# A hybrid encoder block on one core: the last output projection in one row of matmuls, both tiles' transposes and expert choices behind it

## The reference

```python
x = x + merged @ w_out[l]
x = x + moe_ffn(rms_norm(x, norm_ffn[l]), w_router[l], b_router[l], w_gate[l], b_gate[l], w_up[l], b_up[l], w_down[l], b_down[l])
...
logits = (xt @ w_router + b_router).astype(jnp.float32)
top_val, top_idx = lax.top_k(logits, TOP_K)
wts = jax.nn.softmax(top_val, axis=-1)
...
g = xblk @ w_gate[e] + b_gate[e]
u = xblk @ w_up[e] + b_up[e]
...
return act @ w_down[e] + b_down[e]
```

## Time and profile before

| | before |
|---|---|
| median of 3 runs | 1459.51 us (1458.72 to 1461.27) |
| the profiled execution: its own time | 1459.15 us |
| its span, first to last instruction | 1457.0 us |
| TensorE busy | 1426.1 us (98%) |
| VectorE busy | 592.2 us (41%) |
| ScalarE busy | 405.9 us (28%) |
| GpSimd busy | 63.5 us (4%) |
| granted TensorE clock, mean | 1.000 |
| data moved | 491.27 MB, mean 337 GB/s |

### The profile page before, as it was taken

The page is one execution under the profiler, slowest core; times in us unless marked ns, Lnnn a source line. Parts: engine busy times, 40 slices in busy tenths (PEclk is TensorE's granted clock), DMA queues, the critical chain, the costliest instruction groups (busy, mean ns, idle before and its releaser), DMA issues.

```text
span 1457.0 us, 18622 instructions
## 1 busy us (share of the span) xinstructions
PE 1426.1 (98%) x7575; PEld 820.1 (56%) x7575; DVE 592.2 (41%) x1149; ACT 405.9 (28%) x601; POOL 63.5 (4%) x50
## 2 busy tenths in 40 slices
PE   6999999999999999999999999999999999999998
PEld 6898888777778873444444444444444444433443
DVE  6779788787778552112121121211112111111111
ACT  5766666556535441010110110001011010101110
POOL 5110000111100000000000000000000000000000
PEclk9999999999999999999999999999999999999999
DMA  7455444654563969999999999999999999999996
GB/s 248 153 186 177 155 138 161 196 160 160 173 244 131 379 261 423 428 428 427 429 428 430 428 429 428 429 429 428 429 428 429 428 429 428 429 428 429 428 427 287
DMA packets 74001, 491.27 MB, mean 337 GB/s; under 512 B 5265, under 2 KB 8977, under 8 KB 49377
## 3 DMA queue, kind: packets, MB, share of 16 engines
q1 hardware_dynamic: 71280, 487.57, 82.8%
q10 hardware_dynamic: 2160, 2.62, 0.6%
q0 software_dynamic: 512, 0.43, 0.2%
HBM read 488.93 MB, written 1.07 MB: 336 GB/s over the span
## 4 chain that ended last, share of the span: by engine, by line
PE 80%; DMA 10%; DVE 6%; ACT 2%; issue 2%; DVEq 0%; ACTq 0%; SPq 0%
PE ps L1929 26%; PE ps L1967 13%; PE ps L1590 7%; PE ps L1857 7%; PE ps L1592 7%; PE ps L1591 7%; DMA regions<-in_w_up 6%; PE ps L1577 4%; PE ps L1909 4%; DMA regions<-in_w_gate 3%; DVE regions L1165 2%; DVE splits L1019 2%; PE ps L1804 1%; ACT splits L706 1%; PE ps L1937 1%
## 5 line engine op out<-in xcount | busy, mean ns | idle before, releaser
L1929 PE MATMUL ps<-regions,sig 128*64 128x512 f32 x2048 | 463.4, 594 | 4.5 <-DMA regions<-in_w_gate 4.2
L1929 PEld LDWEIGHTS ps<-regions,sig 128*64 128x64 f32 x2048 | 141.9, 137 | 277.1 <-issue 259.5
L1967 PE MATMUL ps<-regions,tmp 128*64 128x512 f32 x1024 | 225.1, 592 | 0.0
L1590 PE MATMUL ps<-splits,regions_r 128*128 128x512 f32 x512 | 205.8, 402 | 1.9 <-DVE regions_r L1012 1.7
L1592 PE MATMUL ps<-splits,regions_r 128*128 128x512 f32 x512 | 200.1, 391 | 0.0
L1591 PE MATMUL ps<-splits,regions_r 128*128 128x512 f32 x512 | 199.8, 390 | 0.0
L706 ACT ACTIVATE splits<-halves 128x1024 fp32r<-128x1024 f32 x152 | 159.1, 1056 | 100.2 <-PE ps L1592 83.4
L1019 DVE TENSOR_TENSOR splits<-halves,splits 128x1024 fp32r<-128x1024 f32 x132 | 166.0, 1262 | 46.5 <-ACT splits L706 45.1
L892 ACT ACTIVATE work<-work 128x512 f32<-128x512 f32 x32 | 20.1, 629 | 475.4 <-DVE work L1517 475.4
L1967 PEld LDWEIGHTS ps<-regions,tmp 128*64 128x64 f32 x1024 | 71.8, 137 | 131.9 <-issue 129.5
L1857 PEld LDWEIGHTS ps<-craw,regions 128*128 128x128 f32 x1024 | 119.2, 192 | 25.6 <-issue 25.2
(11 more groups left out here) (299 smaller groups left out, 1186.3 us busy)
## 6 DMA issues: line engine op xcount, KB each, us to landing
regions<-in_w_gate SPq DMA_DIRECT2D x64, 2048.0 KB, 29.7
regions<-in_w_up SPq DMA_DIRECT2D x64, 2048.0 KB, 28.0
regions<-in_w_down SPq DMA_DIRECT2D x64, 2048.0 KB, 30.9
halves<-in_w_in SPq DMA_DIRECT2D x48, 1024.0 KB, 5.2
halves<-in_w_br_b SPq DMA_DIRECT2D x8, 1024.0 KB, 5.1
halves<-in_w_mem_kv SPq DMA_DIRECT2D x8, 1024.0 KB, 5.0
halves<-in_w_br_a SPq DMA_DIRECT2D x4, 1024.0 KB, 7.5
halves<-in_w_br_c SPq DMA_DIRECT2D x4, 1024.0 KB, 7.5
```

The lines of the kernel that those rows point to most:

```text
L1590: pe.matmul(out, lhs[0], rhs[0], start=start, stop=False, skip_group_check=True)
L1929: last = pe.matmul(ps[64 * h:64 * h + 64, bank, :], xgT[:, 4 * k + c], eslots[slot][:, c, h * NB:(h + 1) * NB], start=(k == 0 and c == 0), ...
L1967: last = pe.matmul(ps[64 * h:64 * h + 64, D_BANK, :], actT[:, c, 64 * k:64 * k + 64], eslots[slot][:, c, h * NB:(h + 1) * NB], start=False ...
```

## The change

The four quarters of the second tile are now steps of the list: `second(0)` and `second(1)` behind unit first("wo", 1) + 1, `second(2)` and `second(3)` behind the last unit. So PE's projection is one row of 48 matmuls: the first tile's quarters 0 and 1, the second tile's 0 and 1, then the same of quarters 2 and 3. `outT` and `logits` come behind it, `outT` with both `turn_out` groups in it. On DVE the step `outT` begins with `add_out(0)`, `norm_begin(0)`, `norm_end(0)` (the root's inversion, split from `choose`) and `add_out(1)`; then come all copies, `norm_begin(1)`, `norm_end(1)`, `choose(0)`, `find_first(0)`, `choose(1)`. PE waits for `logits_taken` of tile 0 before `last_logits(1)`. The router's weights are scaled (`router_scale`) behind unit first("bc", 0) + 1 in place of with ("wo", 0). No instruction of a tile is added or left out, and the streams of ACT and SP are the same. The diff, cut (the functions `add_out`, `take_xT`, `norm_begin`, `second_tile` and `turn_out` only move up in the file, unchanged):

```diff
     at(first("wo", 1), "picks")
-    at(first("wo", 1) + 2, "outT")
-    at(first("wo", 1) + 3, "logits")
+    for q in range(2):
+        at(first("wo", 1) + 1, "second", q)
+        at(first("wo", 1) + 3, "second", q + 2)
+    at(UNITS, "outT")
+    at(UNITS, "logits")
+    at(first("bc", 0) + 1, "router_scale")
...
+            def norm_end(t):
+
+                inverse_root(rs_2[:, t:t + 1]).then_inc(sem("second_norm"), 1)
+                dve.wait_ge(sem("second_norm"), t + 1)
...
+                elif kind == "router_scale":
+
                     dve.wait_ge(gain2_landed, 32)
...
                 elif kind == "outT":
+                    add_out(0)
+                    norm_begin(0)
+                    norm_end(0)
+                    add_out(1)
                     for c2 in range(2):
...
             def choose(t):
 
-                inverse_root(rs_2[:, t:t + 1]).then_inc(sem("second_norm"), 1)
-                dve.wait_ge(sem("second_norm"), t + 1)
                 dve.wait_ge(sem("logits_ready"), t + 1)
...
-            add_out(0)
             take_xT(0)
-            norm_begin(0)
-            choose(0)
-            add_out(1)
             take_xT(1)
             norm_begin(1)
+            norm_end(1)
+            choose(0)
             find_first(0)
             choose(1)
...
+                elif kind == "second":
+                    second_tile(step[1])
...
                     for c2 in range(2):
                         by_columns(lambda t: x_sb[:, t], c2)
+                    turn_out(0)
+                    turn_out(1)
...
-            second_tile(0)
-            turn_out(0)
-            second_tile(1)
             last_logits(0)
-            second_tile(2)
-            second_tile(3)
-            pe.wait_ge(gemm_taken, GEMM_AT[("wo", 1, 0)] + 1)
+            pe.wait_ge(gemm_taken, GEMM_END)
             open_sum(0, 0)
-            turn_out(1)
+            pe.wait_ge(sem("logits_taken"), 1)
+            last_logits(1)
 
             b = group()
             pe.wait_ge(sem("chosen_ready"), 1)
             pe.matmul(ps[:, b, 0:EXPERTS], upto_r[:], chosen_r[:, 0], start=True, stop=True).then_inc(misc_ready, 1)
-            pe.wait_ge(gemm_taken, GEMM_END)
             open_sum(1, 0)
-            last_logits(1)
```

More of the change, by code:

```diff
@@ L967, in rstd_here, with add_out, take_xT, norm_begin @@
                 return last
+            across = [P, TOP_K, EXPERTS]
+            def add_out(t):
+                n = GEMM_AT[("wo", 1, t)]
+                if t == 0:
+                    dve.wait_ge(sem("wo_first_tile"), 1)
+                else:
+                    dve.wait_ge(unit_used, UNITS)
+                dve.tensor_tensor(x_sb[:, t, NB:2 * NB], x_sb[:, t, NB:2 * NB], ps[:, GEMM_BANKS[n % 4], :], ALU.add)\
+                    .then_inc(gemm_taken, 1)
+            def take_xT(t):
+                b = group()
+                dve.tensor_copy(xT[:, 4:8, t * P:(t + 1) * P], ps[:, b, :].rearrange("p (c t) -> p c t", c=4))\
+                    .then_inc(misc_taken, 1)
+            def norm_begin(t):
+                dve.wait_ge(sem("out_squares"), TT + t + 1)
+                link(dve.tensor_tensor(ss_2[:, t:t + 1], ss_part[:, t:t + 1], ss_part[:, TT + t:TT + t + 1], ALU.add))
+                variance(rs_2[:, t:t + 1], ss_2[:, t:t + 1], D)
+            def norm_end(t):
+                inverse_root(rs_2[:, t:t + 1]).then_inc(sem("second_norm"), 1)
+                dve.wait_ge(sem("second_norm"), t + 1)
             dve.wait_ge(sem("masks"), 3)
@@ L1599, in router, with second_tile, turn_out @@
                 return last
+            def second_tile(q):
+                w = first("wo", 1) + q
+                hi, lo = quarter(w)[1:]
+                b = GEMM_BANKS[GEMM_AT[("wo", 1, 1)] % 4]
+                for c in range(2):
+                    k = 2 * q + c
+                    last = three_passes(ps[:, b, :], (mergedT[0][:, k, P:T], mergedT[1][:, k, P:T]),
+                                        (hi[:, c], lo[:, c]), k == 0, k == KC - 1)
+                last.then_inc(unit_used, 1)
+            def turn_out(t):
+                b = group()
+                pe.wait_ge(gemm_taken, GEMM_AT[("wo", 1, t)] + 1)
+                for c in range(4):
+                    last = turn(ps[:, b, c * P:(c + 1) * P], x_sb[:, t, (4 + c) * P:(5 + c) * P])
+                last.then_inc(misc_ready, 1)
             pe.wait_ge(sem("masks"), 3)
@@ L1826, in _ @@
                         by_columns(lambda t: merged[:, t], c2)
-            def second_tile(q):
-                w = first("wo", 1) + q
-                hi, lo = quarter(w)[1:]
-                b = GEMM_BANKS[GEMM_AT[("wo", 1, 1)] % 4]
-                for c in range(2):
-                    k = 2 * q + c
-                    last = three_passes(ps[:, b, :], (mergedT[0][:, k, P:T], mergedT[1][:, k, P:T]),
-                                        (hi[:, c], lo[:, c]), k == 0, k == KC - 1)
-                last.then_inc(unit_used, 1)
-            def turn_out(t):
-                b = group()
-                pe.wait_ge(gemm_taken, GEMM_AT[("wo", 1, t)] + 1)
-                for c in range(4):
-                    last = turn(ps[:, b, c * P:(c + 1) * P], x_sb[:, t, (4 + c) * P:(5 + c) * P])
-                last.then_inc(misc_ready, 1)
             def last_logits(t):
```

17 lines of the change are left out of this document (removed).

## The result

| | before | after |
|---|---|---|
| median of the runs shown with the result | 1459.35 us (20 runs, 1458.36 to 1461.27) | 1466.07 us (20 runs, 1459.58 to 1472.85) |
| ratio, 95% interval | | 1.0039 [1.0028, 1.0051] |
| profiled execution | 1459.15 us, mean clock 1.000 | 1471.44 us, mean clock 0.991 |

What follows compares the result with a forecast made beforehand. It took a full-rate stream of expert loads, paced from the expert loop's start, as the bound. 1459.15 + 1.5 for new waits, other terms at 0, gave 1460.65, or 1461.0 against the median; range 1458.9 to 1463.6.

Steps and rivals of the forecast that it cites:

- The clock: In the rearranged stretch behind the projection the granted clock was to stay full at 2.4 GHz, with no loss taken.
- Rival D: The clock falls to 1.2 GHz behind the new wait, costing 6 to 12 us, 1467 to 1473 us; chance 0.02.
- Size of a fall: Some 12.5 us of PE work between 529.2 and 543.4 at 1.2 GHz would cost 6 to 12 us.
- load (2, 2): Ninth load of the expert stream, held until PE frees its slot; taken as the later limit by about 0.3 us.
- The new wait: Before turn_out(1), PE idles 1.2 us because add_out(1) and the copies stand behind tile 0's root on DVE.
- The root of tile 0: On ACT behind the projection, the root follows its table load at once at 529.2, freeing DVE about 530.4.
- rival A: Tile 0's root comes later still, delaying the add, copies, router and loop: up to 1463.3 us; chance 0.13.
- At full clock: Waits between projection and gathers make take_gathered, the expert loop and the end 1.5 us later.
- The early load (1, 0): On SP's queue this load goes 5.5 us earlier but gains nothing, hidden behind the slot of load (2, 2).
- One to one: At the expert loop, any later start moves the kernel's end by the same amount, here 1.5 us.
- the stream's start: Rival limit on the expert loads: earlier loads would carry the end up to 3.9 us earlier, 1455.6; chance 0.04.

Runs made afterwards that it cites:

- F4: The kernel before with two more TensorE waits, for tile 1's squares before the first open_sum and tile 1's norm before open_sum(1, 0): 1469.45 us, ratio 1.0062.
- F1: The changed kernel with twelve extra transposes (result unused) in TensorE's wait before turn_out(1): 1466.85 us, ratio 1.0039.
- E1: The changed kernel with two extra 512-column matmuls (four passes, result unused) between turn_out(0) and turn_out(1): 1459.96 us, ratio 1.0010.
- F3: The kernel before with 28 extra transposes in a row behind the projection's last matmul: 1461.02 us, ratio 1.0012.
- G2: The kernel before with 16 extra router products (32 passes of 32 columns) behind the projection's last matmul: 1461.37 us, ratio 1.0015.
- K1: G1 with open_sum(0, 0) moved into the wait before turn_out(1) and open_sum(0, 1) between the router's products: 1463.53 us, ratio 1.0025.
- G1: The changed kernel with its four open_sum placed singly between the router's products and the ranks, no work added: 1461.18 us, ratio 1.0017.
- J1: E1 with load (1, 0) released together with load (1, 1), 5.5 us later: 1460.36 us, ratio 1.0003.
- E5: The kernel before with one more TensorE wait, for tile 1's squares before its first open_sum: 1460.86 us, ratio 1.0013.
- J2: The kernel before with load (1, 0) released together with load (1, 1), some 3.6 us later: 1461.50 us, ratio 1.0013.
- A2: The changed kernel again, with no edit, on another chip: 1467.71 us, ratio 1.0044.
- E2: The changed kernel with DVE's add_out(1) and the two outT copies moved ahead of norm_end(0): 1467.79 us, ratio 1.0062.
- E3: The changed kernel with outT's eight transposes back between the projection's units and the router's first eight products ahead of turn_out: 1467.45 us, ratio 1.0054.
- G3: As E3, with the router's first eight products inside the projection too: 1465.76 us, ratio 1.0035.
- H4: The changed kernel with E1's two extra matmuls right behind the projection, ahead of all transposes: 1461.84 us, ratio 1.0026.
- F2: The changed kernel with open_sum(0, 0) and open_sum(0, 1) moved into the wait before turn_out(1): 1466.89 us, ratio 1.0043.

## Why the prediction was wrong

**The clock: the step that failed.** The prediction took no loss there, with the reasons that the granted clock "remains so where transposes, router and short waits alternate, in the very stretch that is rearranged", and that eight transposes in a row had shown no fall. Both sentences are true of before and neither says how near that stretch stood to a fall. F4 shows it: two waits more, in the unchanged order, and five of six runs fall. Rival D had the mechanism with its size, 1467 to 1473 us "behind the new wait"; the falling runs measured 1466.04 to 1472.85. It got a chance of 0.02, and 11 of 20 runs were of that kind: the term that the sum put at nothing measured 5.7 to 12.5 us in each of them (above the median of the full-clock runs), with the clock at 0.50 from 536.4 to about 556.9 in the one that was profiled. The range to 1463.6 left it out.

What the row of eight transposes could not show is the sum of the parts. The old order lays the light work between matmuls of the projection and puts an `open_sum` between any two of the router's and the transposes' groups. The new order puts the projection ahead, and behind it come 16 transposes, 24 router passes (12 products), and only then the first 512-column passes, with 1.31 us of idleness in the midst. The Trainium skill ("TensorE: Matmul & The Clock Gate", "Part 4: PE-mode transpose") says that transposes don't count for the clock as matmuls do. By that rule the prediction should have given rival D far more. F1, with twelve more transposes in the wait and 8 falls in 12, agrees with it against E1; F3 and G2, with 3 us of nothing but thin work and no fall, show that it decides nothing by itself.

**Size of a fall.** The prediction had "half of it again and more, 6 to 12 us". The fall of the profiled execution lasts from 536.4 to about 556.9. I had let it end at 543.4, the forecast start of the loop; it takes in both gathers and the first products of expert 0 as well. At +5.7 to +12.5 against the full-clock median 1460.39 the runs cover the whole of that. F1's profiled execution against E1's gives 8.3 us at load (2, 2) and 9.7 in the whole time for such a fall of 20 us. K1's fall of 10 us began later and cost less; of G1's falls no trace was taken.

**The new wait: right.** Predicted: 1.2 us of idleness before `turn_out(1)`, released by DVE's first copy, behind an `add_out(1)` that starts 1.2 us after the projection's end. Measured: 1.31, released by L1407, with the add at 531.68 and the projection's end at 530.24, 1.4 ahead of it. That end was forecast at 529.2; in this execution the short fall at 434 us moved all that follows, so the differences are to be compared, not the times.

**The root of tile 0: right, and rival A falls.** The root starts at 530.47, right behind its table load (529.18 + 1.28), so nothing is hidden in the 1.84 us of the earlier trace rows. The Trainium skill ("ScalarE: Activation LUTs", "What ACT_TABLE_LOAD costs") puts a drain of 1.38 us behind such a load; this row shows none, as the earlier trace rows at 540.49 had not.

**At full clock: near, with one term missing.** +1.5 us was forecast. The nine full-clock runs gave 1460.39, +1.04 against the median before, and E1, at the same point of the order, +1.14. The early load (1, 0) is worth nothing (J1), as said. The forecast put load (2, 2) near 570.2, and E1 has it at 570.29. What came out smaller is the step from there to the end.

**One to one: wrong by about a microsecond of slack.** I had written that the end hangs on the loop's start "microsecond for microsecond", since the slot of load (2, 2) was the later of two limits "by a little". In the profiled executions with full clock from 530 us on, the time stands behind the issue of load (2, 2) by:

| kernel | issue of (2, 2), us | time, us | difference |
|---|---|---|---|
| before | 568.67 | 1459.15 | 890.5 |
| G1 | 569.60 | 1459.45 | 889.9 |
| E1 | 570.29 | 1459.75 | 889.5 |
| J1 | 570.44 | 1460.05 | 889.6 |
| G2 | 571.84 | 1461.36 | 889.5 |
| F3 | 571.85 | 1461.14 | 889.3 |
| E5 | 572.27 | 1461.66 | 889.4 |
| J2 | 570.53 | 1463.35 | 892.8 |

In the six of them whose loop was delayed, the slot comes 0.9 to 3.6 us later than before and the end follows one to one at 889.3 to 889.9. The kernel before stands 0.6 to 1.2 above that. So there something other than the slot was the later limit, by about a microsecond, and a delay of the loop costs that much less: F3's slot is 3.2 later and its execution 2.0 (its median +1.56), G2's 3.2 and 2.2 (+1.75), E1's 1.6 and 0.6. E5's slot is 3.6 later because its trace has the short fall at 434 as well as its wait of 1.62. J2 says that the other limit is the stream's start: it delays only the first load, by some 3.6 us, and stands at 892.8. Why its median is only 1.75 above before and not all of the 3.6 stays open. So +1.5 came near the measured +1.0 with a slot term that was right and a slack that was put at nothing.

**What stays open.** The runs show which orders fall and which don't, not what the chip counts. Whether transposes and router products count less than 512-column passes each for their time, or whether it is idle moments within them that the trace doesn't show, was not told apart. Nor did any run show why one execution of the changed kernel falls and the next does not, or why the old wait at 432 us brings a short fall in some executions.

| kernel | what stands between projection and gathers | runs that fall |
|---|---|---|
| before with 28 transposes, or 16 router products (F3, G2) | 3 us more thin work, all four `open_sum` behind | 0 of 22 |
| before with one wait (E5) | 1.62 us idle | 0 of 11 |
| before with two waits (F4) | 1.63 and 2.35 us idle | 5 of 6 |
| change (with A2) | 1.31 us idle, thin work in a row | 15 of 25 |
| the wait moved behind the router (E2) | 1.89 us idle, thin work in a row | 6 of 6 |
| light work partly inside the projection again (E3, G3) | 0.22 and 1.17, or 0.51, 0.89 and 0.48 us idle | 9 of 10 |
| its wait filled with transposes (F1) | no wait, thin work | 8 of 12 |
| four long-rowed passes added at the start (H4) | no wait | 5 of 12 |
| the same added in the middle (E1, J1) | no wait before the ranks | 0 of 21 |
| `open_sum` moved into the wait (F2) | 0.47 us idle behind the router | 5 of 5 |
| long-rowed work spread (G1) | 1.31 us idle | 3 of 11, at less cost |
| spread, and one in the wait (K1) | 0.45 us idle in the wait, 0.46 ahead of the gather | 9 of 11, at less cost |

## What to carry to other kernels

Transposes, router products and small waits that lay among long matmuls were covered twice here, in time and in clock; before you bundle the matmuls and leave the light work behind them, ask what TensorE's clock will do there, and give that rival the chance that its size deserves, since the falling runs here cost 5.7 to 12.5 us where the wait itself lasted 1.31. Full clock in the profile of before said nothing of the margin. When you compare two traces, look for low clock outside the changed stretch too: here a short fall 100 us ahead of it made up about 1.4 of the 12.3 us. When a kernel's runs come in two groups, look at each run's mean clock before you look for a cause in the waits, and judge a remedy by the share of runs that fall, in ten or more of them.

## What the runs showed that I had not expected

- The clock fell to half with TensorE busy 2.00 of 2.00 us in every stretch since the projection (F1), and with four 512-column passes at the start of the stretch (H4, 5 of 12).
- Adding 1.7 us of useless matmuls made the changed kernel 6 us faster (1459.96 against 1466.07, with 1458.82 and 1459.35 before), and moving useful ones into the same place did nothing (F2, 1466.89).
- A fall is decided per execution: the same program on one chip took 1460.18 or 1469.76 us (F1).
- The loads pass it all on: with the clock down at 434 to 437 and at 536 to 557, the slot of load (2, 2) came 11.3 us later and the end 12.3 us later, although TensorE has 7.1 us in hand at the end by the expert's pace.
